# A three-tap filter of the Conformer stage moved from GpSimd to ScalarE and VectorE

## The reference

```
h = depthwise_conv(a * jax.nn.sigmoid(b), lp['conf_dw_w'], lp['conf_dw_b'])   # 31 taps
mu = mean(h, -1); var = mean((h - mu)**2, -1)
hn = (h - mu) * rsqrt(var + EPS) * conf_ln_g + conf_ln_b
silu(hn) @ w_br_conf
```

```
ph = depthwise_conv(ph, lp['hy_short_w'], lp['hy_short_b'])    # 3 taps, 1536 channels
v, x1, x2 = jnp.split(ph, 3, axis=-1)
```

## Time and profile before

| | us |
|---|---|
| median of 3 runs | 6575.56 (6571.24 to 6582.12) |
| the profiled execution, its own time | 6576.75 |
| its span, first to last instruction | 6575.0 |
| context stage, layer 0 | 559.5 to 650.2 of the span |
| latent stage, layer 0 | 1292.5 to 1448.5 |
| latent stage, layer 1 | 4525.0 to 4680.9 |

### The profile page before, as it was taken

The page is one execution under the profiler, slowest core; times in us unless marked ns, Lnnn a source line. Parts: engine busy times, 40 slices in busy tenths (PEclk is TensorE's granted clock), DMA queues, the critical chain, the costliest instruction groups (busy, mean ns, idle before and its releaser), DMA issues. The chain is left out here.

```text
span 6575.0 us, 70842 instructions
## 1 busy us (share of the span) xinstructions
PE 5364.0 (82%) x24102; PEld 4110.2 (63%) x24102; DVE 4381.9 (67%) x7631; ACT 1713.7 (26%) x2926; POOL 987.2 (15%) x696
## 2 busy tenths in 40 slices
PE   7786888888877648888888877988897468999998
PEld 5385776335656537666666745843366357999997
DVE  1347523773368789999999963248543896777776
ACT  0132321201235412222222212112022463333333
POOL 0003000140000024444444410004100001111110
PEclk8897999889987779999999988988998668999999
DMA  5141322011225459999999932211112237777775
GB/s 202 68 147 64 109 70 81 19 70 39 77 91 160 122 195 390 387 389 392 388 389 388 392 141 80 84 51 38 64 58 75 51 80 247 276 272 273 277 272 195
DMA packets 445188, 1177.50 MB, mean 179 GB/s; under 512 B 223180, under 2 KB 256237, under 8 KB 375855
## 3 DMA queue, kind: packets, MB, share of 16 engines
q1 hardware_dynamic: 371314, 638.83, 28.6%
q0 software_dynamic: 73728, 536.90, 21.0%
HBM read 1112.72 MB, written 62.91 MB: 179 GB/s over the span
## 5 line engine op out<-in xcount | busy, mean ns | idle before, releaser
L1832 POOL DMA_INDIRECT arena<-in_peer_uv,kept x512 | 749.8, 1464 | 3557.8 <-POOLq L1733 1815.7
L215 PE MATMUL psum<-v_ring_hi,w_hi 128*128 128x512 f32 x1536 | 643.0, 419 | 251.9 <-DVE w_lo L1924 251.9
L215 PE MATMUL psum<-h_hi,u_ring_hi 128*128 128x384 f32 x2048 | 698.7, 341 | 10.1 <-DVE ring_lo L1903 4.4
L215 PE MATMUL psum<-h_hi,ring_lo 128*128 128x384 f32 x2048 | 692.8, 338 | 0.0
L215 PE MATMUL psum<-h_lo,u_ring_hi 128*128 128x384 f32 x2048 | 692.0, 338 | 0.0
L1947 DVE SCALAR_TENSOR_TENSOR arena<-arena 128x1024 f32<-128x1024 f32 x512 | 635.1, 1282 | 19.5 <-issue 0.5
L215 PE MATMUL psum<-ring_lo,w_hi 128*128 128x512 f32 x1536 | 629.4, 410 | 0.0
L215 PE MATMUL psum<-v_ring_hi,w_lo 128*128 128x512 f32 x1536 | 625.2, 407 | 0.0
L1935 DVE CUSTOM_DVE_ANT_0 arena<-arena 128x1024 f32<-128x1024 f32 x512 | 604.9, 1218 | 0.0
L1875 ACT ACTIVATE u_ring_hi<-kept 128x1024 fp32r<-128x1024 f32 x256 | 271.5, 1061 | 963.5 <-DMA kept<-in_peer_u 957.1
L215 PEld LDWEIGHTS psum<-v_ring_hi,w_hi 128*128 128x128 f32 x1536 | 303.0, 197 | 350.6 <-issue 289.8
(11 more groups left out here) (325 smaller groups left out, 9946.8 us busy)
## 6 DMA issues: line engine op xcount, KB each, us to landing
kept<-in_mix SPq DMA_DIRECT2D x312, 512.0 KB, 3.2
kept<-in_peer_u SPq DMA_DIRECT2D x256, 512.0 KB, 6.2
kept<-in_peer_uv SPq DMA_DIRECT2D x256, 512.0 KB, 4.7
kept<-in_ada SPq DMA_DIRECT2D x96, 512.0 KB, 4.3
gate_scratch<-arena SPq DMA_DIRECT2D x12, 4096.0 KB, 20.9
arena<-gate_scratch SPq DMA_DIRECT2D x128, 384.0 KB, 7.6
arena<-in_k_dft_x SPq DMA_DIRECT2D x6, 2048.0 KB, 14.5
spec_scratch<-arena SPq DMA_DIRECT2D x4, 2048.0 KB, 8.5
```

Of the source, the lines that this page charges most:

```text
L215: done = pe.matmul(out, lhs[x], rhs[y], start=first and j == 0, stop=last and j == 2)
L1832: pool.indirect_dma_start(rows[q % NBUF], None, peer_uv, bass.IndirectOffsetOnAxis(ap=row_id[q % G][:, q // G:q // G + 1], axis=0))\
```

## The change

The GpSimd list of the stage is gone, and the tile `part` with it. The first tap of the short filter (product and bias) is now 12 activations of ScalarE with the function identity, a weight and a bias per partition, ahead of its gates; a new semaphore `short_begun` tells VectorE when they are done. The other two taps are 12 scalar_tensor_tensor each on VectorE, with the running sum as second operand: the second tap stands between the subtraction of the mean and the wait for the root, the third between the last merge and the wait for the sigmoid. The arithmetic is the same but for the rounding of a fused product and sum.

```diff
-            part = area(a + 10752, T)
+            short_w, short_b = par_of("hsw"), par_of("hsb")
...
+                    for c in range(12):
+                        last = act.activation(hs[:, c, :], m["hp"][:, c, 0:T], ACT.Identity, scale=short_w[:, c:c + 1],
+                                              bias=short_b[:, c:c + 1])
+                    last.then_inc(short_begun.sem, 1)
                     with act.Fori(0, 3) as i:
                         for k in (0, 2):
                             gate(i, k)
...
+                    def short_tap(tap):
+                        for c in range(12):
+                            dve.scalar_tensor_tensor(hs[:, c, :], m["hp"][:, c, tap:tap + T], short_w[:, tap * 12 + c:tap * 12 + c + 1],
+                                                     hs[:, c, :], ALU.mult, ALU.add)
...
                     dve.tensor_tensor(hc, hc, ps[:, 4, 0:T].unsqueeze(1).broadcast_to([P, 4, T]), ALU.subtract).then_inc(dve_a.sem, 1)
+                    dve.wait_ge(short_begun.sem, short_begun.at(1))
+                    short_tap(1)
                     dve.wait_ge(root_ready.sem, root_ready.at(1))
                     dve.reciprocal(rs, rs)
...
                     merge(3, 3)
+                    short_tap(2)
                     dve.wait_ge(act_a.sem, act_a.at(2))
                     dve.tensor_tensor(hc, hc, sg, ALU.mult)
 
-                @block.gpsimd
-                def _(pool):
-                    w, b = par_of("hsw"), par_of("hsb")
-                    for c in range(12):
-                        pool.tensor_scalar(hs[:, c, :], m["hp"][:, c, 0:T], w[:, c:c + 1], b[:, c:c + 1], ALU.mult, ALU.add)
-                    for tap in (1, 2):
-                        for c in range(12):
-                            pool.drain()
-                            pool.tensor_scalar(part, m["hp"][:, c, tap:tap + T], w[:, tap * 12 + c:tap * 12 + c + 1], None, ALU.mult)
-                            pool.drain()
-                            pool.tensor_tensor(hs[:, c, :], hs[:, c, :], part, ALU.add)
```

More of the change, by code:

```diff
@@ L99, in build @@
         rows_free, dots_ready, gelu_ready = new("expert_rows_free"), new("dots_ready"), new("small_gelu_ready")
+        short_begun = new("short_filter_begun")
         a_ready, a_free, o_done = new("hidden_ready"), new("hidden_read"), new("outputs_done")
@@ L1130, in stage_conformer @@
             gate_ready.add(8)
+            short_begun.add(1)
             streamed(16, 16)
```

## The result

| | median us | runs | ratio to the kernel before, 95% interval |
|---|---|---|---|
| before | 6573.40 | 4 | |
| changed | 6526.41 (6517.05 to 6540.64) | 4 | 0.9928 [0.9907, 0.9949] |
| changed, timed again (`e1_after_again`) | 6512.85 (6507.66 to 6528.54) | 5 | 0.9900 [0.9887, 0.9914] |
| forecast | 6516.5, range 6506 to 6538 | | 0.9910 |

The change makes the kernel 0.7 to 1.0% faster; 0.9% was forecast. The forecast ratio lies inside both intervals. The two medians lie on either side of the forecast time: 6526.41 is within the wide range but above the forecast's own range of 6509 to 6524, and 6512.85 is inside both. The profiled execution took 6517.05 us, its span is 6515.2 us (6575.0 before).

A forecast was written before the change was run, and what follows sets the result against it. VectorE, slowed by GpSimd's work beside it, sets the loop's pace, with TensorE close behind. Latent 30.7 - 6.8 = 23.9, twice 47.8, plus context 16.0 - 4.7 = 11.3: 59.1 us less, 6516.5 us at the median, range 6506 to 6538.

The forecast's parts named there:

- What slows VectorE is GpSimd: In the latent stage: a 128x512 multiply-add takes 1177 ns beside GpSimd's work, 776 ns after its last instruction.
- Rival (c): VectorE's taps don't get faster without GpSimd, so only the tails are paid: 6594 us, slower; chance 0.04.
- TensorE becomes the bound of the latent loop, VectorE stays it in the context: Loops before the mean: the first mean comes 30.7 us sooner in each latent stage, 16.0 us in the context.
- The context's mean: Context stage: TensorE's last pair takes 8.67 us, so the mean starts at 619.7 in place of 635.70.
- Rival (a): Latent loop: five TensorE pairs still cost 15.7 us each, losing 9.8 us a stage: 6536 us; chance 0.09.
- the loss at the start: Start of each latent stage: TensorE's first two pairs start as before and take 29.75 us, later ones 13.74 each.
- ScalarE's tap costs nothing: Start of the stage: twelve added activations take 8.5 us, hidden under 14 us of cover.
- The second tap is hidden, the third paid: Latent tail: 8.1 us fit the 8.73 us wait before the reciprocal; twelve before the last multiplication cost 6.8 us.
- Rival (b): Stage tails: the added multiply-adds don't fit the waits and all 24 are on the path: 6540 us; chance 0.05.
- Nothing follows or is given back: After the stages: no DMAs move and the Fourier stage shifts as a whole; together 59.1 us are gained.
- the latent tails: From the mean to the end of each latent stage: the added multiply-adds cost 6.8 us.
- the context's: Context tail: the added multiply-adds cost 0.5 us before the reciprocal and 4.2 before the last multiplication, 4.7 in all.

The follow-up runs named there:

- e1_after_again: The changed kernel with no edit, timed again in five rounds; 6512.85 us, ratio 0.9900 to the kernel before.
- e6_three_taps_less: The changed kernel without three of the Conformer's 31 taps (12 multiply-adds in all); 6515.48 us.
- e3_no_second: The changed kernel without the short filter's second tap, the 12 multiply-adds ahead of the reciprocal; 6511.07 us in a single execution.
- e10_e7_again: The changed kernel with all 24 added multiply-adds ahead of the root in the latent stages, timed a second time; 6501.27 us, ratio 0.9882.
- e8_mean_earlier: The kernel with all 24 multiply-adds ahead of the root, with the means also moved earlier in the latent stages; 6503.99 us, ratio 0.9889.

## Why the prediction was right

Point by point, forecast against the latent stage of layer 1 and the context:

- *What slows VectorE is GpSimd.* Shown: taking its work away gives 2.74 us for four from the first round on, putting it back beside the new work gives 1122 ns for one and a kernel slower than before. Rival (c) falls. One reading was off: 4.7 us is four times the mean of one, but four in a row overlap, and the rows of the timeline between 1310 and 1391 give 4.2 to 4.9, 4.5 on average. The sum doesn't use the 4.7.
- *TensorE becomes the bound of the latent loop, VectorE stays it in the context.* Shown by `e6_three_taps_less`: 0 and 5.6 us. This was the step that kept the forecast from 35 us a stage, as VectorE alone would give: VectorE's loop ends 93.8 us into the stage (forecast 93.6), TensorE's mean starts at 98.5 (98.7; 129.3 before), so 30.9 us against 30.7. In the context the mean starts at 59.8 (60.2), 16.4 against 16.0.
- *The context's mean: near the number, by another path.* The forecast let TensorE's last pair set it, at 8.67 us as behind a gap of 2.71 us. In the changed kernel the pair took 7.14 us behind its gap of 1.99, and VectorE's last tap released the mean ([0.67 <-DVEq L1108] above). Twice the forecast's path was the true one: in `e3_no_second` and `e10_e7_again` the pair took 8.83 us behind 1.99 and 2.00 us, and the mean started at 60.6. The trace of before had a warning, 7.17 us for a pair behind a gap of 2.79:

```profile
592.10 7.17 PE L1034 MATMUL psum<-arena,kept 128*128 128x256 f32 x32 [2.79 <-DVE arena L1080]
```

That the two paths end within a microsecond of each other is luck, and it is why the wrong one cost the forecast only 0.4 us.

- *TensorE's clock.* Rival (a) wanted 15.7 us a pair. The 224 matmuls took 98.30 us in one piece, 0.98 of the clock, with the loss at the start that was counted. (Not every pair behind a gap had cost 15.7 before: the first one, behind 5.79 us, took 17.02.) The Fourier stage started behind a gap of 12.89 us in place of 6.41 and its first 64 matmuls took 29.78 us (29.67 before): the longer gap costs 0.1 us.
- *ScalarE's tap costs nothing.* 8.57 us (forecast 8.5), no table load, the first gate of the latent stage still released by TensorE. The estimate worked out from the figures of the Trainium skill (ScalarE: Activation LUTs, "What ACT_TABLE_LOAD costs" and "Table sets") was 8.6 us for the twelve. The trace now agrees with it, and with the identity needing no table load of its own. Against GpSimd's first tap this move is worth some 1.6 to 2.4 us, all in the context.
- *The second tap is hidden, the third paid.* 8.04 us in a wait of 8.8, then 8.03 bare. The whole tail costs 6.5 us in a latent stage (forecast 6.8) and 4.2 in the context (4.7). Rival (b) falls with `e3_no_second`.
- *Nothing follows or is given back.* The sum of the stages fell by 61.0 us (59.1 forecast), the span by 59.8. The medians can't confirm the sum that closely: under the medians of before that were taken with them, they are 47.0 us lower in the first four runs and 64.6 in the second set, while the stages are alike in both profiles. That one median fell on either side of the forecast time is chance.

The terms that were off are small and have one sign: the latent tails were 0.3 us too dear each and the context's 0.5, the latent means came 0.2 us sooner and the context's 0.4. Together they make the 1.9 us.

Still open: what makes the stretch of the experts vary by 15 us between executions, why the clock fell behind a gap of 2 us in some executions and not in others, and why the multiply-add beside the second set of GpSimd instructions is 55 ns quicker than beside the first.

## What to carry to other kernels

An engine whose result nobody waits for can still set the time, through the engine that it slows: look at the same instruction's mean before and after that engine's last instruction, not only at who waits for whom. A slowed engine's gain is capped by the engine that is next behind it, so write out both schedules to the end; here the cap took 35 us down to 31, and its other side was 5 us of new slack, into which the added work should go: with the same 24 instructions all moved into waits, the two latent stages were together 11.6 us shorter, and 10.7 when timed again. Price added work by the wait in front of which it stands, place by place: twelve instructions were free in one wait and cost 6.3 us in the next.

## What the runs showed of the hardware

- VectorE's scalar_tensor_tensor of 128x512 with two SBUF tensors: 747 ns alone, 1177 beside GpSimd's tensor_scalars and tensor_tensors, 747 beside its memsets. Single-input tensor_scalars suffer from both: four take 1.91 us alone, 3.13 beside GpSimd's tensor_scalars and 3.04 beside its memsets.
- The merges, which read one tensor from PSUM and one from SBUF, are not slowed: 677 ns for the four beside GpSimd, 686 for the six without it, both from the groups of VectorE:

```profile
L1080 DVE TENSOR_TENSOR arena<-psum,arena 128x512 f32 x4 | 2.7, 677 | 0.0
```

```profile
L1085 DVE TENSOR_TENSOR arena<-psum,arena 128x512 f32 x6 | 4.1, 686 | 0.0
```

- GpSimd's memset is short: 60 of 128x512, each behind a drain, took 38.8 us.
- What a gap of TensorE of some 2 us does to its clock differs from run to run. Behind 2.10 us in `e8_mean_earlier` the granted clock stayed at 1.00. Behind 1.99 us in the context stage the same pair took 7.14 us at 1.00 in the changed kernel, and 8.83 in `e3_no_second`, with the clock at 0.50 for part of it. In the latent stage of layer 0 before, five gaps of 0.87 to 8.57 us were followed by pairs of 17.02, 15.70, 15.85, 15.70 and, behind 0.87, 13.97 us.
- TensorE starts a latent stage behind 6.4 us without work at a granted clock of 0.50. The seven pairs that follow without a gap took 98.30 to 99.15 us, by how long that lasts.
